# Two-pass MLP of a Trainium2 trunk step: order of the weights' low halves, the second weight load, the residual reload and the last block's adds

## What is computed

```python
h = _rms_norm(x, norm_mlp[i]) * (1.0 + sc2) + sh2
x = x + g2 * (jnp.square(jax.nn.relu(h @ mlp_w1[i])) @ mlp_w2[i])
...
return _rms_norm(x, final_norm), jnp.stack(states, axis=1)
```

## Time and profile before

| what | value |
|---|---|
| median of 3 runs | 2529.99 us (2527.24 to 2534.19) |
| time of the profiled execution | 2525.03 us |
| span of its trace | 2522.5 us |
| PE busy in the span | 97% |
| DVE, POOL, ACT busy | 61%, 41%, 31% |

### The profile page before, as it was taken

How to read it: one execution, slowest core, us unless ns; L and a number is a source line. 1 busy time by engine, 2 the same in 40 slices (tenths; PEclk the granted TensorE clock), 3 DMA queues, 4 the chain that set the end, 5 groups by cost and what they waited for, 6 DMA issues and landing times.

```text
span 2522.5 us, 39010 instructions
## 1 busy us (share of the span) xinstructions
PE 2441.2 (97%) x14100; PEld 2141.8 (85%) x14100; DVE 1544.1 (61%) x2527; ACT 792.5 (31%) x1244; POOL 1028.1 (41%) x552
## 2 busy tenths in 40 slices
PE   7999999978999999999999999899999999999998
PEld 3988899977888888888888888787888888888887
DVE  6635752265368767777767776577333336767764
ACT  3311122133152222232232231664333334423322
POOL 7125322153113343333333333025565657776740
PEclk9999999989999999999999999999999999999999
DMA  7424533276201212111212112022434346343322
GB/s 252 153 79 147 167 101 107 109 234 218 77 18 59 100 58 75 58 58 60 98 62 71 58 58 75 17 105 85 147 108 144 110 165 237 119 148 116 125 84 84
DMA packets 153348, 274.12 MB, mean 109 GB/s; under 512 B 7428, under 2 KB 105512, under 8 KB 152232
## 3 DMA queue, kind: packets, MB, share of 16 engines
q1 hardware_dynamic: 150288, 263.22, 30.6%
q10 hardware_dynamic: 2968, 9.63, 1.2%
HBM read 204.66 MB, written 63.96 MB: 106 GB/s over the span
## 4 chain that ended last, share of the span: by engine, by line
PE 85%; DVE 6%; issue 3%; ACT 2%; POOL 2%; DMA 1%; ACTq 0%; POOLq 0%; SPq 0%; DVEq 0%
PE bank L457 79%; PE bank L2250 1%; PE bank L2403 1%; DMA ada_st_in<-in_ada_w_dram 1%; PE bank L2315 1%; PE bank L2278 1%; DVE X L1716 0%; POOL qsF L1586 0%; DVE ada_acc_in L1708 0%; DVE h1L L1882 0%; DVE vtok L1762 0%; DVE G3L L2134 0%; DVE ada_acc_mlp L1708 0%; DVE xgm L1875 0%; POOL ringL L1574 0%
## 5 line engine op out<-in xcount | busy, mean ns | idle before, releaser
L1716 DVE SCALAR_TENSOR_TENSOR X<-bank,mod,X 128x512 f32<-128x512 f32 (+1 forms) x852 | 544.9, 685 | 262.2 <-PE bank L457 261.8
L1371 POOL TENSOR_TENSOR ringL<-stage,ringH 128x2048 fp32r<-128x2048 f32 x66 | 314.1, 4758 | 591.8 <-ACT ringH L831 563.3
L457 PE MATMUL bank<-hH,ringH 128*128 128x512 f32 (+1 forms) x1248 | 446.2, 358 | 0.2 <-DVE hL L1882 0.2
L457 PE MATMUL bank<-hL,ringH 128*128 128x512 f32 (+1 forms) x1248 | 442.0, 354 | 0.0
L457 PE MATMUL bank<-hH,ringL 128*128 128x512 f32 (+1 forms) x1248 | 441.8, 354 | 0.0
L457 PEld LDWEIGHTS bank<-hH,ringH 128*128 128x128 f32 x1248 | 236.3, 189 | 33.7 <-DVE hL L1882 1.0
L457 PEld LDWEIGHTS bank<-hH,ringL 128*128 128x128 f32 x1248 | 236.0, 189 | 33.0
L457 PEld LDWEIGHTS bank<-hL,ringH 128*128 128x128 f32 x1248 | 236.2, 189 | 32.2
L831 ACT ACTIVATE ringH<-stage 128x2048 fp32r<-128x2048 f32 x65 | 124.0, 1908 | 313.4 <-PE bank L457 311.9
L457 PE MATMUL bank<-ringH,hH 128*128 128x256 f32 x640 | 184.1, 288 | 5.4 <-DVE hL L1685 5.4
L457 PE MATMUL bank<-ringL,hH 128*128 128x256 f32 x640 | 181.9, 284 | 0.0
(11 more groups left out here) (377 smaller groups left out, 5748.9 us busy)
## 6 DMA issues: line engine op xcount, KB each, us to landing
stage<-in_mlp_w_dram SPq DMA_DIRECT2D x64, 1024.0 KB, 5.7
ada_st_mlp<-in_ada_w_dram SPq DMA_DIRECT2D x18, 1536.0 KB, 8.2
stage<-in_ev_w_in_dram SPq DMA_DIRECT2D x14, 1024.0 KB, 5.1
mid_spill<-midT SPq DMA_DIRECT2D x56, 256.0 KB, 2.2
ada_st_in<-in_ada_w_dram SPq DMA_DIRECT2D x8, 1536.0 KB, 8.9
mid_spill<-midB SPq DMA_DIRECT2D x48, 256.0 KB, 2.0
ada<-in_ada_w_dram SPq DMA_DIRECT2D x8, 1024.0 KB, 13.2
x_spill<-X SPq DMA_DIRECT2D x1, 5120.0 KB, 18.7
```

The costliest lines, as they stand in the source:

```text
L457: mm = nc.tensor.matmul(out, a, b, start=first and n == 0, stop=last and n == 2, skip_group_check=chained)
L1371: nc.gpsimd.tensor_tensor(ringL[slot][:, :], stage[:, :], ringH[slot][:, :].bitcast(F32), ALU.subtract).then_inc(w_lo, 1)
L1716: V.scalar_tensor_tensor(out=X[:, d, cols(t)], in0=src[:, 0:TB[t][1]], scalar=gate_ap, in1=X[:, d, cols(t)], op0=ALU.mult, op1=ALU.add).th ...
```

## The change

No computation is added or removed. Five things are put in another order:

1. POOL's adds of block 1 (`full01`, `full11`) all wait until DVE has made the last `h1L` of block 1; before, each waited only for its own tile.
2. ACT does the relu and square of chunk 1's last two groups (the prompt) ahead of the three high halves of chunk 2's weight sums, not behind them.
3. At the hand-over ACT makes all four weight highs (both parts of both slots), then the `inp`, `inT2` highs and the rest; POOL makes all four weight lows ahead of the eight sums.
4. SP reads `X` back in four pieces, of 3, 1, 2 and 2 feature tiles, not in three of 3, 3 and 2; the second weight load (c = 1) stands behind the first two of them, as before, which are now 4 tiles and not 6. DVE waits for the first 4 tiles and the last 4 separately.
5. The load of `fin`, the final norm's gain, goes behind the loads of pair 1.

```diff
@@ block.sync
-        for i, p in enumerate(("5", "6", "7")):
+        for p, ds, signal in (("5", slice(0, 3), x_kept), ("6", slice(3, 4), x_kept), ("7", slice(4, 6), x_again),
+                              ("7", slice(6, 8), x_again)):
             sp.wait_ge(m_mm, first_mm(last) + M_AT[p])
-            if i == 2:
+            if ds.start == 4:
                 w2_load(0, 1)
-            ds = slice(3 * i, min(3 * i + 3, DT))
             sp.wait_ge(x_kept, 32)
-            sp.dma_start(X[:, ds, :], x_dram[:, ds, :]).then_inc(x_again, 16)
+            sp.dma_start(X[:, ds, :], x_dram[:, ds, :]).then_inc(signal, 16)
...
-        sp.dma_start(fin[:, :], final_norm.rearrange("(o d) -> o d", o=1).to_broadcast([P, D])).then_inc(fin_in, 16)
...
         second_loads(0)
+        sp.dma_start(fin[:, :], final_norm.rearrange("(o d) -> o d", o=1).to_broadcast([P, D])).then_inc(fin_in, 16)
@@ block.scalar, second_pass
-            w2_high(s, 0, 1)
-            w2_high(s, 1, 1)
+            if not isinstance(s, int) or s > 0:
+                w2_high(s, 0, 1)
+                w2_high(s, 1, 1)
@@ block.scalar
+        plain_group(1, 4)
+        plain_group(1, 5)
         for i in (1, 2, 3):
             sum1_hi(2, i)
-        plain_group(1, 4)
-        plain_group(1, 5)
...
         w2_high(0, 1, 0)
+        w2_high(0, 0, 1)
+        w2_high(0, 1, 1)
         mid_high(0, "p")
@@ block.gpsimd, quarter_add
-            pool.wait_ge(h_lo, GRP * 2 + DT * (1 + tb) + d + 1)
+            pool.wait_ge(h_lo, GRP * 3 if tb == 1 else GRP * 2 + DT + d + 1)
@@ block.gpsimd, second_pass
-            w2_low(s, 0, 1)
-            w2_low(s, 1, 1)
+            if not isinstance(s, int) or s > 0:
+                w2_low(s, 0, 1)
+                w2_low(s, 1, 1)
@@ block.gpsimd
-        w2_low(0, 0, 0)
-        w2_low(0, 1, 0)
+        for part in range(2):
+            w2_low(0, 0, part)
+            w2_low(0, 1, part)
@@ block.vector, second_pass
-                        dve.wait_ge(x_again, 16 * 3)
+                        if d0 + d < HD:
+                            dve.wait_ge(x_kept, 16 * 4)
+                        else:
+                            dve.wait_ge(x_again, 16 * 2)
```

## The result

| | before | after |
|---|---|---|
| median, 14 runs each on the same chip | 2529.31 us (2524.46 to 2535.70) | 2533.05 us (2529.99 to 2542.30) |
| profiled execution, its span | 2525.03, 2522.5 | 2536.23, 2533.4 |

The ratio is 1.0020, 95% interval 1.0011 to 1.0029: about 5.1 us slower, 2.8 to 7.3. It is an estimate over the runs of both kernels and not the quotient of the two medians, which lie 3.74 us apart (1.0015). The forecast was 3.7 us more, 2533.7, and no difference of 0.3%. So the change costs a little, and the measurement can just tell it from nothing.

What follows compares the result with a forecast made beforehand. PE was taken as the bound nearly everywhere, so only its waits at the block scheme's start (+2.6 us) and the hand-over (+1.1) counted: +3.7 on the median 2529.99 gave 2533.7 us, range 2525 to 2540.

Steps and rivals of the forecast that it cites:

- The adds, G2F at 1720.4: Block 1's norm: eight bunched POOL adds start at 1704.2, alternating with DVE; G2F ends at 1720.4, 4.5 us late.
- exclusive: Rival: each POOL and DVE alternation takes 1.98 us, not 1.70; +8.1 us in all, 2538.1; chance 0.14.
- The Trainium skill's lock: Rule weighed: DVE and GpSimd lock a shared port pair for whole instructions; an add and a subtraction would take 1.98 us.
- G4F 4.2 to 4.3 late: DVE after the adds: 20 ops and POOL's next_sums follow, so G4F's part 1 starts at 1741.4, 4.2 to 4.3 us late.
- ACT's order, 1.66: End of chunk 1 on ACT: the prompt's squares ahead of three qsH save 1.66 us before the relu PE awaits.
- First place: Start of the block scheme: late G4F less ACT's saving, +4.25 - 1.66 = +2.6 us; PE waits some 9 us.
- Hand-over: First high 1.9 us earlier, sums end later at 2112.9; "pb" waits for inT1L instead of ringL: +1.1 us, bounds +0.4 to +1.8.
- The low clock, taken as unchanged: Behind PE's waits: the low granted clock, worth 1.7 us, stays in the sum at the hand-over since PE still waits.
- The sum: Whole kernel: 2.6 at the block scheme's start plus 1.1 at the hand-over, +3.7 us, everything else at nothing.
- Gate open: Rival at the hand-over: "pb" follows "pa" at once, -5.3 and -1.7 us; total -4.4, 2525.6; chance 0.10.

Runs made afterwards that it cites:

- adds_only: The kernel before with only the adds of block 1 bunched (the change's point 1); 2532.66 us, ratio to before 1.0018.
- t1_late_before: The kernel before with DVE's inT1L moved behind the updates of "pa"; one run, 2525.44 us beside 2527.56 for before.
- t1_late: The changed kernel with DVE's inT1L moved behind the updates of "pa"; 2527.36 us, ratio to before 0.9993.
- best1: The changed kernel with the adds unbunched, inT1L behind the updates of "pa", and G4F's part 1 ahead of G2L and G3L on DVE; 2520.56 us, ratio to before 0.9966.
- adds_back: The changed kernel with each add of block 1 waiting for its own tile again; 2533.52 us, ratio to before 1.0024; timed again 2526.26 us, 0.9992.
- prompt_first: The kernel before with only ACT's new order for the prompt (the change's point 2); 2525.76 us, ratio to before 0.9988.
- best2: The kernel of best1 with the adds of block 1 bunched as in the changed kernel; 2525.60 us, ratio to before 0.9987.
- best2_again: The same kernel as best2, run once more; one run, 2517.64 us beside 2527.59 for before.
- best1_again: The same kernel as best1, timed once more; 2520.43 us, ratio to before 0.9964.

## Why the prediction came out right, point by point

- **The adds, G2F at 1720.4.** Measured 1720.66. The eight adds took 12.76 us where 1.3 + 7 x 1.70 = 13.2 was forecast: 1.64 for an add and a subtraction, and the "exclusive" rival with 1.98 is out at this place. The norm ended where it was said (last h1L at 1704.26 on the clock of before, forecast 1704.2).
- **The Trainium skill's lock** (SBUF — State Buffer, "SBUF: two separate sides"), exclusive and held for the whole instruction, holds in its kind and not in its sum. xgm, which reads PSUM, was never stretched (0.75 with adds and without), and ops with two SBUF inputs were. But two engines that took turns needed less than both ops after each other, 1.64 and not 1.98 us, and the measurement decides.
- **G4F 4.2 to 4.3 late.** Measured 4.22 against the profile that the forecast was worked out from. Which op meets next_sums changed (G1L, not G3L), and the price did not: 10.21 against 10.02. adds_only has the whole term by itself, +4.20 in A. That profile had the low clock of 1706:1710 in it, though, which put next_sums later; against t1_late_before the adds cost 4.58, so the close agreement is in part luck.
- **ACT's order, 1.66.** Measured 1.57 (6.91 to 5.34), 1.55 from adds_only to after, and alone 1.92 against before and 1.54 against t1_late_before. First place +2.6 forecast, +2.65 measured; PE's wait 8 to 9 us, measured 8.55.
- **Hand-over.** The first high started 1.96 us earlier behind the midB relu, forecast 1.9. The sums ended 3.19 later, forecast 3.2 (21.82 us behind midB, 18.63 before). Here two errors cancelled: the sums began 4.2 later (10.81 and 6.60 behind midB), where - 1.9 + 4.7 = 2.8 was forecast, and took 11.0 us and not the 12.0 of before. "pb" started 25.90 us behind it and not 24.62, +1.28, forecast +1.1; C as a whole is +1.09 (+0.7 to +1.5 against the four kernels with the old hand-over). The gate is inT1L, as t1_late shows by opening it. Not seen: a wait of 1.81 us ahead of "pa". Four ringL in a row stretch inpL and inT2L to 3.42 us each (2.55 and 2.31 before), and the eight updates of X behind them come late. It costs nothing in the changed kernel, since "pb" waits anyway, but it is what t1_late and best1 are left with.
- **The low clock, taken as unchanged.** This is the mis-sized term. Behind 8.55 us of waiting the first 4 us had 0.50 and not 0.57, and B is 0.46 longer. Its larger side shows only in the experiments: in adds_back and prompt_first the low clock at the scheme's start vanished, worth 1.6 us in B. By my text it could go only with the wait; it went when the wait was still 1.73 us long.
- **The sum:** +3.7 forecast, +4.2 in the stretches, 5.1 [2.8, 7.3] by the ratio. The terms are +2.65, +0.46 and +1.09. The medians lie 3.74 apart; that they meet the forecast to a tenth is luck, since the stretches and the interval don't tell it so closely. "Gate open" had "pb" right behind "pa" only as a rival; with t1_late's edit this comes true, at 5.07 under the changed kernel. Its price, 5.3 + 1.7 = 7.0 under before at the hand-over, was too high: C of t1_late is 3.98 under before, with a wait of 1.81 us ahead of "pa" and one of 0.70 behind it.

What stays open: why the clock was lower in the first set of adds_back, what lets POOL hold DVE off in best2, and what parts 4 and 5 are worth by themselves. Neither was undone alone; that the second load no longer holds ACT up is read from the traces (its first high starts 1.17 us behind midB in the changed kernel).

## What to carry to other kernels

An addition that is bunched to spare one loop is paid where its consumer starts: look at what the next engine in line wants first, and put that op, not the tidy group, ahead (best1 moved G4F's part 1 and left the adds where they were). When a wait is taken from one releaser, look in the same list for the next one before moving work; here the same edit of DVE's list was worth 5 us after the move and nothing before it. Compare kernels by the stretches between marks in unchanged work, since a repeated kernel gave the same stretches within 0.1 us (but for the one stall of best2) where its medians moved by 0.3%. One profile of before isn't enough for that either: the same instructions gave A of 53.73 and 53.35, and C of 363.70 to 364.08.

## What the runs showed of the hardware

- **Low clock behind a wait** (1.00 is 2.4 GHz throughout, 0.50 is 1.2). In the same place of the program, PE's wait and the granted clock of the next 4 us were: 0.47 us and 1.00 (best1), 1.73 and 1.00 (adds_back), 1.76 and 1.00 (prompt_first), 2.06 and 0.57 (before), 3.26 and 0.60 (t1_late_before), 3.73 and 0.50 (best2_again), 8.55 and 0.50 (after), 10.11 and 0.62 (adds_only). The price is what B shows: 345.4 with the clock up, 346.8 to 348.0 without. It isn't a matter of the length of the wait alone. Ahead of "pa" at the hand-over PE waited 1.81 us in after, adds_back and t1_late, and the next 4 us had 1.00; in best1 it waited 1.82 us at the same place, behind the same instructions, and the window 2109.20:2113.20 had 0.62. In 1706:1710, behind waits of 0.34, 0.95 and 0.93 us in before and 0.33, 0.95 and 0.95 in t1_late_before, it was 0.57 and 1.00, with the same program up to there.
- **One op of DVE can stand for 14.12 us** under ten ops of POOL, where the same program at the same distance took 1.94 us in another execution. The other way round, one sum of POOL stood for 7.71 and 7.70 us under some twelve ops of DVE (best1, best1_again); there the two executions agree.
